# Expert layers: a first round of ten gather places, four query steps moved into the first unit, and a reordered head

## The reference, cut to what matters

```
q = (hf @ w_query).reshape(T, PEER_HEADS, 2, PEER_HALF)          # 8 heads x 2 halves x 128
scores = jnp.einsum("thpd,hpnd->thpn", q, sub_keys)              # 128 keys per half
top_v, top_i = lax.top_k(scores, PEER_TOPK)                      # 16 of each half
cand_v = top_v[:, :, 0, :, None] + top_v[:, :, 1, None, :]
cand_i = top_i[:, :, 0, :, None] * PEER_NKEYS + top_i[:, :, 1, None, :]
best_v, best_pos = lax.top_k(cand_v, PEER_TOPK)                  # 16 of 256 pairs
expert_idx = jnp.take_along_axis(cand_i, best_pos, axis=-1)
gates = jax.nn.softmax(best_v, axis=-1)
...
u = jnp.take(expert_u, idx, axis=0)                              # one row of 1024 per choice
vv = jnp.take(expert_v, idx, axis=0)
a = jax.nn.gelu(jnp.einsum("td,thkd->thk", h, u))
return jnp.einsum("thk,thkd->td", g * a, vv)
```

## Time and profile before

| | us |
|---|---|
| median of 3 runs | 2331.65 |
| the profiled execution | 2338.47 |
| its span | 2336.9 |
| TensorE (matmul) busy | 2099.3 (90%) |
| VectorE busy | 1598.8 (68%) |
| ScalarE busy | 805.5 (34%) |
| GpSimd busy | 569.1 (24%) |
| DMA share of queue q0 (the gathers) | 61.1% of 16 engines' span |

### The profile page before, as it was taken

One profiled execution on the slowest core, in us unless ns is written; L12 is line 12 of the kernel. 1 busy time (PEld: TensorE's weight loads), 2 busy tenths in 40 slices (PEclk: granted clock), 3 DMA queues, 4 the chain that ended last, 5 costly groups with the idle time before them and its releaser, 6 DMA issues.

```text
span 2336.9 us, 25022 instructions
## 1 busy us (share of the span) xinstructions
PE 2099.3 (90%) x8877; PEld 1362.0 (58%) x8877; DVE 1598.8 (68%) x3313; ACT 805.5 (34%) x1745; POOL 569.1 (24%) x613
## 2 busy tenths in 40 slices
PE   8999999999999999987888877999999987777877
PEld 6699977899897665543333333687665543333333
DVE  6788955788857486776676675566586667657755
ACT  5654463544455333122212113455232212221122
POOL 0100010000003034333333343011143333333431
PEclk9999999999999999998999899999999999999998
DMA  7188933598764579999999999854699999999997
GB/s 282 68 317 336 341 123 109 188 360 328 286 216 145 198 310 422 421 421 422 421 421 421 422 421 421 334 176 161 253 380 422 421 421 421 421 421 421 421 421 304
DMA packets 161917, 772.30 MB, mean 330 GB/s; under 512 B 13672, under 2 KB 14056, under 8 KB 90128
## 3 DMA queue, kind: packets, MB, share of 16 engines
q0 software_dynamic: 80640, 587.24, 61.1%
q1 hardware_dynamic: 81168, 183.67, 22.0%
HBM read 769.76 MB, written 1.11 MB: 330 GB/s over the span
## 4 chain that ended last, share of the span: by engine, by line
PE 53%; DMA 32%; DVE 9%; issue 2%; ACT 2%; POOL 1%; another core or an unknown queue 0%; POOLq 0%; SPq 0%; DVEq 0%; ACTq 0%
DMA ring<-in_experts_uv_dram,experts_at 17%; PE experts_first L3170 9%; PE experts_fourth L3170 8%; DMA experts_v_slot<-in_experts_uv_dram,experts_at 7%; DMA experts_spare<-in_experts_uv_dram,experts_at 4%; PE mix_sums L233 3%; PE mix_sums L235 3%; PE mix_sums L234 3%; PE mlp_hid L233 2%; PE mlp_hid L235 2%; PE mlp_hid L234 2%; PE mlp_acc L233 2%; PE mlp_acc L234 2%; PE mlp_acc L235 2%; DMA mlp_ada_rows<-in_ada_turned_dram 2%
## 5 line engine op out<-in xcount | busy, mean ns | idle before, releaser
L3021 ACT ACTIVATE experts_diagonal<-ident,experts_weight 128x128 f32<-128x128 f32 x488 | 155.9, 390 | 634.3 <-DVE experts_weight L2891 618.6
L2637 POOL DMA_INDIRECT ring<-in_experts_uv_dram,experts_at x248 | 239.8, 967 | 369.8 <-PE experts_first L3170 193.6
L3170 PE MATMUL experts_first<-ring,experts_diagonal 128*128 128x512 f32 x560 | 268.4, 629 | 46.3 <-ACT experts_diagonal L3021 46.2
L228 DVE TENSOR_TENSOR early_w_lo<-ring,early_w_hi 128x1024 fp32r<-128x1024 f32 x196 | 243.2, 1261 | 95.7 <-ACT early_w_hi L2284 52.7
L3170 PE MATMUL experts_fourth<-ring,experts_diagonal 128*128 128x512 f32 x432 | 213.7, 645 | 51.8 <-ACT experts_diagonal L3021 51.8
L2836 DVE CUSTOM_DVE_ANT_0 ring<-ring,experts_third 128x1024 f32<-128x1024 f32 x140 | 171.0, 1221 | 101.9 <-DMA ring<-in_experts_uv_dram,experts_at 101.1
L3170 PEld LDWEIGHTS experts_first<-ring,experts_diagonal 128*128 128x128 f32 x560 | 109.9, 201 | 186.2 <-issue 128.0
L3170 PE MATMUL experts_fourth<-experts_v_slot,experts_diagonal 128*128 128x512 f32 x368 | 172.8, 613 | 36.9 <-ACT experts_diagonal L3021 34.0
L2836 DVE CUSTOM_DVE_ANT_0 ring<-ring,experts_second 128x1024 f32<-128x1024 f32 x108 | 131.9, 1221 | 89.3 <-DMA ring<-in_experts_uv_dram,experts_at 87.1
L3170 PEld LDWEIGHTS experts_fourth<-ring,experts_diagonal 128*128 128x128 f32 x432 | 87.0, 206 | 174.6 <-issue 111.2
L2836 DVE CUSTOM_DVE_ANT_0 experts_v_slot<-experts_v_slot,experts_second 128x1024 f32<-128x1024 f32 x92 | 112.3, 1221 | 88.0 <-DMA experts_v_slot<-in_experts_uv_dram,experts_at 88.0
(11 more groups left out here) (555 smaller groups left out, 4700.6 us busy)
## 6 DMA issues: line engine op xcount, KB each, us to landing
mlp_ada_rows<-in_ada_turned_dram POOLq DMA_DIRECT2D x48, 1024.0 KB, 8.1
ring<-in_w_in_dram SPq DMA_DIRECT2D x19, 2048.0 KB, 8.8
ring<-in_mlp_w_in_dram SPq DMA_DIRECT2D x16, 2048.0 KB, 11.4
ring<-in_mlp_w_out_dram SPq DMA_DIRECT2D x16, 2048.0 KB, 13.3
ring<-in_gla_w_in_dram SPq DMA_DIRECT2D x6, 2048.0 KB, 9.2
ring<-in_w_out_dram SPq DMA_DIRECT2D x4, 2048.0 KB, 7.8
ring<-in_w_query_dram SPq DMA_DIRECT2D x4, 2048.0 KB, 8.1
experts_v_slot<-in_w_query_dram SPq DMA_DIRECT2D x4, 2048.0 KB, 13.0
```

The lines of the kernel that those rows point to most:

```text
L228: return dve.tensor_tensor(out_lo, a, hi.bitcast(F32), ALU.subtract)
L2637: pool.indirect_dma_start(pair(i), None, rows, bass.IndirectOffsetOnAxis(ap=at[:, n, j:j + 1], axis=0)).then_inc(pair_in[slot[i]], 16)
L3021: act.activation(diagonal[:, i % TOPK, :], K.ident[:], ACT.Copy, scale=weight[:, n, i % TOPK:i % TOPK + 1]).then_inc(diagonal_ready, 1)
L3170: mm = pe.matmul(y[n // PH][:, b, :], diagonal[:, j, :], v_row(i)[:, b * HALF:(b + 1) * HALF], start=n % PH == 0 and j == 0, stop=False, s ...
```

## The change

It has six parts, all in `experts`:

1. `START` no longer holds p0a and p0b: the first round of gathers has ten places instead of twelve. Gather 10 then goes into the place of gather 0 (u_first) and waits for its `v_used`, where it went into p0a and waited for twelve query steps (`q_done`). p0a and p0b come in at gather 22, p1a and p1b at gather 56 instead of 24. So there are 10 places up to gather 21, 12 up to gather 55, and 14 from then on; before there were 12 up to gather 23 and then 14.
2. `EARLY` is 8 instead of 12. The four steps of tile 1 with c = 0 to 3 move from the head into the groups of unit 0, and the steps behind them stand in another order (c = 8 to 11 of tile 0 ahead of c = 4 to 7 of tile 1). The late steps take 24 groups instead of 20.
3. On TensorE the steps 0 and 1 are issued in halves (the first four chunks of both, then the last four), step and score alternate from step 3 on, and tile 1's transposes stand behind step 5. The wait for all early scores stands behind the first late step.
4. On ScalarE `square(1, 1)` and `spread(1)` stand behind the copy of query step 2, ahead of the copy of step 3; `gates(0)` (exp, L3007) stands at step 6.
5. ScalarE gets one more instruction, a gelu of one column behind the copy of the queries and scores of the last early step, which loads the gelu table there.
6. `weigh(0)` stands behind dot 4 instead of dot 5.

```diff
-    steps = [(c, t) for first in (0, PH) for t in range(T) for c in range(first, first + PH)]
-    EARLY = PH + 4
-    START = ("u_first", "spare", "out0a", "out0b", "out1a", "out1b", "shared", "extra", "mod", "xn", "p0a", "p0b")
-    LATER = ("p1a", "p1b")
+    steps = ([(c, 0) for c in range(PH)]
+             + [(c, t) for first, t in ((0, 1), (PH, 0), (4, 1), (PH + 4, 0)) for c in range(first, first + 4)]
+             + [(c, 1) for c in range(PH, 2 * PH)])
+    EARLY = PH
+    START = ("u_first", "spare", "out0a", "out0b", "out1a", "out1b", "shared", "extra", "mod", "xn")
+    LATER = {22: ("p0a", "p0b"), 56: ("p1a", "p1b")}
...
-    OPENED = {"p1a": T * PH, 0: T * PH + PH + 4, 1: T * PH + PH + 4, 2: 2 * T * PH, 3: 2 * T * PH}
+    OPENED = {"p0a": PH + 4, "p1a": T * PH + 4, 0: T * PH + PH + 4, 1: T * PH + PH + 4, 2: 2 * T * PH, 3: 2 * T * PH}
...
-        if i == 2 * len(START):
-            queue.extendleft(reversed(LATER))
+        if i in LATER:
+            queue.extendleft(reversed(LATER[i]))
...
-        return {0: 2, 1: 4, 2: 8, 4: T * PH + 4, 6: T * PH + PH, 8: T * PH + PH}.get(n, len(steps))
+        return {0: 2, 1: 4, 2: 8, 4: T * PH, 6: T * PH + PH, 8: T * PH + PH}.get(n, len(steps))
...
         gather(9)
-        pool.wait_ge(q_done, PH + 4)
         for i in range(10, ALL):
...
                     weigh(i // GROUP - 1)
+                if i == GROUP:
+                    weigh(0)
...
         move_queries(2)
-        move_queries(3)
-        move_scores(2)
-        move_scores(3)
         square(1, 1)
         spread(1)
-        gates(0)
-        move_queries(4)
-        move_queries(5)
-        move_scores(4)
-        take_turned(1)
-        copy_h2(1)
-        for s in range(6, EARLY):
+        for s in range(3, EARLY):
             move_queries(s)
+            if s == 5:
+                take_turned(1)
             move_scores(s - 1)
+            if s == 5:
+                copy_h2(1)
+            elif s == EARLY - 2:
+                gates(0)
+            elif s == EARLY - 1:
+                act.activation(std[:, 2 * T:2 * T + 1], K.ident[:, 0:1], ACT.Gelu_apprx_tanh)
         move_scores(EARLY - 1)
...
-        project_step(0)
-        project_step(1)
+        for some in (range(0, KC // 2), range(KC // 2, KC)):
+            project_step(0, some)
+            project_step(1, some)
...
         project_step(2)
-        project_step(3)
-        score(2)
-        score(3)
-        project_step(4)
-        project_step(5)
-        score(4)
-        transposes(1, 0)
-        transposes(1, 1)
-        for s in range(6, EARLY):
+        for s in range(3, EARLY):
             project_step(s)
+            if s == 5:
+                transposes(1, 0)
+                transposes(1, 1)
             score(s - 1)
         score(EARLY - 1)
-        pe.wait_ge(scores_moved, EARLY)
...
                     project_step(late[k])
+                if g == 0:
+                    pe.wait_ge(scores_moved, EARLY)
                 weighted(n, k)
```

4 lines of the change are left out of this document (2 added, 2 removed).

## The result

The change makes the kernel slower by 3.6 us: 2335.00 us median of 22 runs (2331.47 to 2337.41) against 2331.38 for the kernel before in the same set, ratio 1.0016 [1.0010, 1.0022]. Forecast were 2331.0, with 2326.5 to 2337 as the range. The profiled execution took 2335.18 us, its span 2333.6.

The account below looks back on a forecast made before the run. Bound: full DMA stream at 421 GB/s plus one hole per layer. Layer terms of 0 and +0.4 with -0.35 each gave about -0.3 us, 2338.2; less the 6.8 profile-to-median difference, 2331.3, written 2331; range 2326.5 to 2337.

Parts of the forecast that it names:

- the last one of the sum: Whole kernel: the profiled execution's 6.8 us above the median was carried over, turning 2338.2 into 2331.3 us.
- the two holes: One DMA hole per layer, 4.0 and 3.2 us; filling both returns at most 7.2 us, 0.3% of the kernel.
- the first dot comes 4.4 us earlier: VectorE, first layer: square root ahead of the copies starts the first dot at 838.3, not 842.74; second layer 4.0.
- 14.0 + 1.2: First dot to gather 10: 14.0 us of dots, `weigh` and issue, plus 1.2 us for TensorE at half clock.
- the halves: TensorE, steps 0 and 1: hides the wait for VectorE's copy, so all that follows comes 0.8 us earlier.
- the 0.35 for the queue: Stream behind gather 10: short queue costs 0.7 us per layer; the rest of that term counted at half, -0.35 each.
- Rival B: ScalarE's held copy also delays step 5 and the transposes; gather 10 2.9 us later, +6.5 in all, 2338; chance 0.14.
- Rival C: Units 1 to 3: twelve places too few, slow TensorE groups make holes; +2 to +5 us, 2335; chance 0.09.
- The part at half clock: TensorE, first `weighted` after idling: 1.2 us later, between 0 and 2; 2 if the whole first group is slow.
- second hole: DMA stream at gather 14: none expected, by some 1 us; gather 14 at 864.4, stream busy until about 867.
- The hole isn't filled. It moves: First layer's DMA hole: front edge comes 0.8 us earlier, rear edge 0.7.
- Rival A: TensorE warm or overlap small, queue no shorter: gather 10 1.9 and 1.5 us earlier, -3.4, 2328.3; chance 0.22.

Follow-up runs that it names:

- h1_before: The kernel before, unchanged, run and profiled again in the third set; 2329.46 us, profiled at 2328.82.
- i1: The changed kernel plus 20 matmuls with unused results on TensorE ahead of each layer's first `weighted`; 2336.38 us, 1.0026 against the kernel before.
- g1_after: The changed kernel again, unaltered, in the second set on another chip; 2333.27 us, 1.0009 against the kernel before.
- j1_after: The changed kernel once more, unaltered, in the fifth set; 2335.55 us, 1.0018 against the kernel before.
- f3_head: The kernel before with only the head changed (parts 3 to 6), twelve places and twelve early steps kept; 2337.79 us, 1.0005 against the kernel before.
- j2_order: The kernel before with halves, early steps reordered so gathers 10 and 11 wait for eleven, earlier gelu table, score wait moved; twelve places; 2326.37 us, 0.9981.
- i3_before_small: The kernel before with halves, early gelu table, `weigh(0)` behind dot 4 and the score wait moved; twelve places and steps; 2333.24 us, 1.0009.
- g2: The changed kernel with twelve early query steps instead of eight, keeping ten places and the new head; 2341.70 us, 1.0039 against the kernel before.
- f2_places: The kernel before with only the ten places (part 1), all twelve early query steps kept; 2347.48 us, 1.0043 against the kernel before.
- i4: The changed kernel with unit 1's choosing behind dots 4 to 7, `weigh(1)` behind dot 8, 14 unused matmuls before the second late step; 2330.56 us, 1.0000.

## Why the prediction was wrong, step by step

**The step that failed** is the last one of the sum, the passage from the profiled execution to the median: "The profiled execution lies 6.8 above the median 2331.65, so I put the same difference on the median." The 6.8 us were no constant that lies on any execution. By h1_before the held copy is worth as much: gather 10 comes 3.8 us later in the first layer (30.60 against 26.79) and 3.0 in the second (29.91 against 26.89), and from gather 0's first packet to gather 255's the layers are 3.75 and 2.99 us longer. The spans of the two profiles differ by 9.7 us (2336.9 and 2327.2): 6.7 in the two layers, 3.3 ahead of the first gather, and 0.3 less between the layers. The first gather goes out anywhere from 818.85 to 825.25 us in the eighteen profiles, whatever the kernel. h1 lies 2.6 us below the median 2331.38, so that the two figures of 6.8 agree so closely is in part chance. The sum compared the changed kernel with a kernel before whose layers were 3 to 4 us longer than those behind its median. With this step fell the sentences that the two holes can return 7.2 us at most (in h1 they hold 0.5) and that the first dot comes 4.4 us earlier: against h1 it is 0.6 from gather 0 (14.69 for 15.33), because there VectorE waits 0.6 us for the square root and not 3.67.

Put on the right base, the prediction's own terms give the right sign. With the first dot at +14.7, as measured, then 14.0 + 1.2: gather 10 at +29.9, where h1 has +26.8. That is 3.1 later, less 0.7 for the halves, and with the 0.35 for the queue 2.75 per layer: +5.5 us. Measured were 2.5 to 5.4 in the four sets, 3.6 in the first comparison. That 2335.0 still lies in the range of 2326.5 to 2337 is luck: its upper part was made for the rivals B and C, and neither is what happened.

**What was right.** Against the profiled execution of before, the changed kernel did nearly what the text says:
- Halves: 0.7 us for 0.8.
- First dot at 14.6 and 14.8 for 15.5. The square root left at 829.81 and VectorE came at 832.07 without a wait: it is its own bound, as said.
- From the first dot to gather 10: 15.65 us for 15.2. The part at half clock was mis-sized: 1.8 us (3.75 against 1.98) for 1.2. PEclk 0.50 there is 1.2 GHz. i1 shows that with TensorE busy ahead of it the same four records take 1.98 us. The Trainium skill (TensorE: Matmul & The Clock Gate, "What's actually happening") has the slow level as the one that an idle engine falls back to. The trace agrees for the first gather's four records; the prediction's reading that the whole first group would be slow went too far, since the second gather took 2.48 us and the next two 3.60 together, as at full clock.
- Gather 10 at 30.3 for 30.7, gather 14 9.95 behind it for 11, the first hole 3.3 and 3.4 us for 4. No second hole is in this profile, but the room is as small as said: in the first layers of g1_after and j1_after gather 14's transfers take 3.71 and 3.92 us instead of 2.49.
- Twelve places in the units 1 to 3 cost nothing: share 1.01 from 872 us on, and no window under 0.99 up to gather 75. Rival C is out.

So gather 10 stands in the changed kernel where it stood in the held execution. "The hole isn't filled. It moves" is true against that one alone; against the median it is made anew.

**Rival A** named warm TensorE as the way to a gain of 3.4 us. i1 built it, and gather 10 moved by the 1.8 us, but the time didn't follow: A has no allowance for gather 14, which VectorE's second weight binds at +40.3. The prediction's "no second hole, by some 1 us" said how little room is there, and A spent it.

**Rival B** saw that the held copy could stay. In the four profiles of the changed kernel it doesn't occur, but three of them are from the other chips, and that of the first isn't on record. In f3_head, which has the same order of the steps 3 to 5 and ran there, it does, in both layers. So the rival isn't refuted for that chip. It never asked the converse, whether the copy is held at all in the runs behind the median. The three times shown (2329.18 to 2333.07) all lay 5 us or more below the profiled one, and the earlier trace rows had in it a wait of 3.91 us with no named releaser: the two belonged together, as h1 shows.

**Where the time goes, then.** With ten places gather 10 has to wait for the first `weighted` and gather 14 for the second; with twelve, gathers 10 and 11 wait only for query steps, and gathers 12 and 16 for the two groups. Two places fewer are 2 x 2.49 = 5.0 us less time for each group. Group 0 opens its first place at +30.34 where h1 has +32.21 (gather 12): 1.9 earlier where 5.0 are needed, 3.1 short. Group 1 opens its first at +40.29 where h1 has +42.64 (gather 16): 2.4 earlier, 2.6 short. The stream loses 2.8 per layer, near both. The 1.9 us are the first dot, 0.6 earlier, and the first weight, 10.88 us behind the first dot instead of 13.97 (a dot sooner, no table load), less the 1.8 of the half clock. The 0.7 of the halves comes back in each layer, and 2 x (2.8 - 0.7) = 4.2 us remain.

**Open.** What holds the copy isn't settled. All four profiles of the first set have it, in both layers, and the first profile of before, whose chip isn't on record; none of the twelve profiles of the other four sets has it, nor the first one of the changed kernel. The timed executions fit: on the first set's chip the 33 of the kernel before took 2333.34 to 2340.44 us, on the two other chips 110 took 2327.48 to 2335.05. This points to the chip and not to the single execution, but one chip against two doesn't show it. Whether the change would be level where the copy is held no run here tells.

## What to carry to other kernels

A profile is one execution. Where its time lies outside the timed runs, don't carry the difference along as a constant: look in it for a wait of that size, above all one whose releaser has no name, and do the sum on a profile that has the median's length. In a ring, write down for each place when it comes free and when the stream needs it; a change pays only where it moves the latest of these, and two places fewer cost two transfers of lead at each of them. j2_order kept all twelve places; it opened the two query places one step earlier, took the gelu's wait off and had the halves.

## What the runs showed of the hardware

- In some profiles ScalarE's copies start late. In the profiled execution of before step 3's matmuls run from 830.59 for 1.95 us, and the copy starts at 834.98, 2.4 us after their end. GpSimd issues six gathers in a row from 829.24 to 836.5 there. In f3_head step 4's copy is the latest, 4.8 us after its step, and starts 2.9 us after the end of the six (a seventh gather is issued between). In h1 the copy of step 3 starts 0.03 us after its step, beside the same six gathers, so they alone don't make it late. The hold also stops TensorE for 2.54 us (before, first layer), and the PEclk of 0.60 at 837.5 in the earlier trace rows follows on that.
- After 5.52 us of idleness the first `weighted` took 3.75 us for its first gather, in all eight layers of the four profiles of the changed kernel; the second gather took 2.48 in the first of them, and from then on it was 1.8 per gather. After 2.66 us of idleness eight records took 5.40 us in the first layer of i3_before_small and 3.70 in its second, and 3.70 after 2.67 us in both layers of i1_after_warm: at this length the gap alone doesn't tell. After 0.5 us (g2) there was no loss.
- A gather that starts on an empty queue behind a hole costs 2.9 to 3.3 us by the trace's packets, and the next one 2.5 to 3.4, against 2.49 in full stream. The two together took up to 1.5 us more than 2 x 2.49 (3.11 + 3.36 in the first layer of f2_places): a hole costs more than its own length, and a second thin place, as in i1 and i4, can give back what the first one saved.
